# Linear attention: 64-row products side by side, and other PSUM banks for the output gate's second layer

## The reference, cut to what matters

```python
b = jnp.cumsum(log_a, axis=3)                       # within a chunk of 64 tokens
qd = q * jnp.exp(b) * (dk ** -0.5)
kd = k * jnp.exp(-b)
kl = k * jnp.exp(b_last - b)
kv = jnp.einsum('bhncd,bhnce->bhnde', kl, v)        # per chunk and head: 128 x 256, sum over 64 tokens
# s_prev[n+1] = decay[n] * s_prev[n] + kv[n]
o_inter = jnp.einsum('bhncd,bhnde->bhnce', qd, s_prev)
a = jnp.where(causal, jnp.einsum('bhncd,bhnsd->bhncs', qd, kd), 0.0)
o = o_inter + jnp.einsum('bhncs,bhnse->bhnce', a, v)
...
o_a = rms_norm(o_a, gla_out_norm) * jax.nn.silu(g_r)   # g_r: the output gate, two layers of 512 columns here
```

## Time and profile before

| what | value |
|---|---|
| median of 3 runs | 1502.66 us (1494.79, 1502.66, 1503.58) |
| the profiled execution's own time | 1496.99 us |
| its span in the trace | 1495.2 us |
| mean granted TensorE clock | 0.966 |
| PE busy | 1289.9 us (86%) |
| DVE busy | 946.0 us (63%) |
| ACT busy | 592.1 us (40%) |
| chain that ended last, by engine | PE 54%, DMA 22%, DVE 12%, ACT 8% |

### The profile page before, as it was taken

One profiled execution on the slowest core, in us unless ns is written; L12 is line 12 of the kernel. 1 busy time (PEld: TensorE's weight loads), 2 busy tenths in 40 slices (PEclk: granted clock), 3 DMA queues, 4 the chain that ended last, 5 costly groups with the idle time before them and its releaser, 6 DMA issues.

```text
span 1495.2 us, 16428 instructions
## 1 busy us (share of the span) xinstructions
PE 1289.9 (86%) x6072; PEld 909.0 (61%) x6072; DVE 946.0 (63%) x1961; ACT 592.1 (40%) x1013; POOL 279.8 (19%) x281
## 2 busy tenths in 40 slices
PE   7998999287878888787878777699899999999998
PEld 7987797243424343342424223397488899999887
DVE  5656455687776868777677765564555456766445
ACT  4455453232322223132322221463445754545334
POOL 1000000244343535443434333000000000000000
PEclk9998899699999999999999999899899999999999
DMA  7442342499999999999999999355234445555551
GB/s 268 136 149 96 113 169 89 175 423 421 421 422 421 415 422 400 421 405 422 403 422 421 421 421 422 151 209 170 85 120 162 142 144 194 167 180 185 202 190 71
DMA packets 56982, 398.78 MB, mean 267 GB/s; under 512 B 7096, under 2 KB 7352, under 8 KB 9032
## 3 DMA queue, kind: packets, MB, share of 16 engines
q0 software_dynamic: 36864, 268.45, 43.5%
q1 hardware_dynamic: 17856, 125.84, 24.2%
q10 hardware_dynamic: 2184, 3.45, 0.7%
HBM read 396.67 MB, written 1.05 MB: 266 GB/s over the span
## 4 chain that ended last, share of the span: by engine, by line
PE 54%; DMA 22%; DVE 12%; ACT 8%; issue 4%; POOL 1%; ACTq 0%; SPq 0%; DVEq 0%; POOLq 0%
PE ps L727 41%; DMA B<-in_ex,eidx 21%; PE ps L970 9%; DVE B L2001 4%; ACT hl L1195 2%; DVE hl L1675 2%; ACT diags L1435 1%; ACT av_ L1430 1%; DVE XT L1684 1%; ACT L1576 1%; ACT L1430 1%; ACT L1417 1%; POOL B L691 1%; DVE av_ L2005 1%; PE ps L930 0%
## 5 line engine op out<-in xcount | busy, mean ns | idle before, releaser
L970 PE MATMUL ps<-B,diags 128*128 128x512 f32 x1024 | 480.4, 615 | 150.0 <-ACT diags L1435 150.0
L970 PEld LDWEIGHTS ps<-B,diags 128*128 128x128 f32 x1024 | 188.9, 193 | 431.3 <-ACT diags L1435 238.5
L1675 DVE TENSOR_TENSOR hl<-ring,hl 128x2048 fp32r<-128x2048 f32 x118 | 270.1, 2291 | 262.4 <-ACT hl L1195 262.2
L691 POOL DMA_INDIRECT B<-in_ex,eidx x256 | 273.7, 1069 | 648.6 <-PE ps L970 358.1
L2001 DVE CUSTOM_DVE_ANT_0 B<-B 128x1024 f32<-128x1024 f32 x256 | 309.8, 1220 | 111.3 <-DMA B<-in_ex,eidx 111.1
L1195 ACT ACTIVATE hl<-ring 128x2048 fp32r<-128x2048 f32 x118 | 224.8, 1908 | 136.4 <-PE ps L727 135.6
L727 PE MATMUL ps<-XT,hl 128*128 128x256 f32 x2136 | 268.4, 287 | 4.2 <-DVE XT L1684 4.2
L727 PEld LDWEIGHTS ps<-XT,hl 128*128 128x128 f32 x2136 | 262.1, 194 | 9.4 <-issue 5.1
L1430 ACT ACTIVATE av_<-av_ 128x2 f32<-128x2 f32 x128 | 26.0, 203 | 430.3 <-DVE av_ L2001 430.3
L727 PE MATMUL ps<-hl,R 128*128 128x512 f32 x792 | 182.7, 391 | 0.0
L727 PE MATMUL ps<-hl,XT 128*128 128x512 f32 (+1 forms) x720 | 164.3, 389 | 7.0 <-DVE B L2086 7.0
(11 more groups left out here) (312 smaller groups left out, 875.6 us busy)
## 6 DMA issues: line engine op xcount, KB each, us to landing
ring<-in_wt SPq DMA_DIRECT2D x117, 1024.0 KB, 4.9
B<-in_ex,eidx POOLq DMA_INDIRECT x256, 13.0
X<-in_x SPq DMA_DIRECT2D x2, 512.0 KB, 4.4
B<-in_mem ACTq DMA_DIRECT2D x1, 1024.0 KB, 10.3
ring<-in_wple SPq DMA_DIRECT2D x1, 1024.0 KB, 5.0
out<-B SPq DMA_DIRECT2D x4, 256.0 KB, 2.0
GB<-in_gffn ACTq DMA_DIRECT2D x1, 512.0 KB, 3.5
GB<-in_gfin ACTq DMA_DIRECT2D x1, 512.0 KB, 4.3
```

The costliest lines, as they stand in the source:

```text
L691: e.indirect_dma_start(out=rows[i % NG][:, :], out_offset=None, in_=A["ex"], in_offset=bass.IndirectOffsetOnAxis(ap=eidx[:, tb, s:s + 1], ...
L970: m = e.matmul(acc[tb][hf][:, :], diags[:, i % 4, :], rows[i % NG][:, 1024 + 512 * hf:1536 + 512 * hf], start=(s == 0), stop=(s == 127))
L1675: e.tensor_tensor(w[1][:, :], ring[:, i % RING, :], w[0][:, :].bitcast(F32), ALU.subtract).then_inc(lo.sem)
```

## The change

Three edits in the linear attention, all on PE and in the planner; no engine other than PE gets another order, and no instruction is added or removed.

- The state products of chunks 0 and 1 are issued together, before the second half of `bq` layer 0: for each pair of heads, both banks are taken, and for each head the product of chunk 0 stands directly before that of chunk 1. `SA(2)` stays between the halves of `gr` layer 1.
- In the outputs the two intra-chunk products of a head stand directly behind each other, and then its inter-chunk products.
- In the deal of banks, two are passed over ahead of `gr` layer 1.

```diff
@@ planner, GROUPS
-        for n in range(3):
-            GROUPS += [(("SA", n, hp), sas[n, hp]) for hp in range(2)]
-            if n == 1:
-                layer_groups("gr", 1, lambda tb: grs[1, tb])
+        GROUPS += [(("SA", n, hp), sas[n, hp]) for hp in range(2) for n in range(2)]
+        layer_groups("gr", 1, lambda tb: grs[1, tb])
+        GROUPS += [(("SA", 2, hp), sas[2, hp]) for hp in range(2)]
@@ planner, the deal
+                if key == ("gr", 1, 0):
+                    turn += 2
                 while turn % 8 in held:
                     turn += 1
@@ PE
-            for n in range(3):
-                o = 64 * (n % 2)
-                for hp in range(2):
-                    ps = bank(("SA", n, hp))
-                    if n == 0 and hp == 0:
-                        e.wait_ge(*klts[1])
-                        e.wait_ge(*gvs[1, 1])
-                    for c in range(2):
-                        h = 2 * hp + c
-                        m = e.matmul(ps[:, c * 256:c * 256 + 256],
-                                     klt[o:o + 64, (n // 2) * 512 + h * 128:(n // 2) * 512 + h * 128 + 128],
-                                     gv[o:o + 64, n // 2, h * 256:h * 256 + 256], start=True, stop=True)
-                    mark(m, ("SA", n, hp))
-                if n == 0:
-                    t_half("bq", 0, 1, XT)
-                else:
-                    t_half("gr", 1, n - 1, XT)
+            def state(n, hp, c):
+                o, h = 64 * (n % 2), 2 * hp + c
+                return e.matmul(ps_of(("SA", n, hp))[:, c * 256:c * 256 + 256],
+                                klt[o:o + 64, (n // 2) * 512 + h * 128:(n // 2) * 512 + h * 128 + 128],
+                                gv[o:o + 64, n // 2, h * 256:h * 256 + 256], start=True, stop=True)
+            e.wait_ge(*klts[1])
+            e.wait_ge(*gvs[1, 1])
+            for hp in range(2):
+                for n in range(2):
+                    bank(("SA", n, hp))
+                for c in range(2):
+                    m = [state(n, hp, c) for n in range(2)]
+                for n in range(2):
+                    mark(m[n], ("SA", n, hp))
+            t_half("bq", 0, 1, XT)
+            t_half("gr", 1, 0, XT)
+            for hp in range(2):
+                bank(("SA", 2, hp))
+                for c in range(2):
+                    m = state(2, hp, c)
+                mark(m, ("SA", 2, hp))
+            t_half("gr", 1, 1, XT)
@@ PE, outputs oN(tb, hp), for each head
                         for q in range(2):
                             n, o = 2 * tb + q, 64 * q
                             m = e.matmul(ps[o:o + 64, c * 256:c * 256 + 256],
                                          AT[o:o + 64, (h * 2 + tb) * 64:(h * 2 + tb) * 64 + 64],
                                          gv[o:o + 64, tb, h * 256:h * 256 + 256], start=True, stop=(n == 0))
+                        for q in range(2):
+                            n, o = 2 * tb + q, 64 * q
                             if n:
                                 e.wait_ge(*sas[n - 1, hp])
                                 m = e.matmul(ps[o:o + 64, c * 256:c * 256 + 256],
```

More of the change, by code:

```diff
@@ L568, in program @@
         MARKS += [("klT", 0), ("klT", 1)]
-        for n in range(3):
-            MARKS += [("SA", n, hp) for hp in range(2)]
-            if n == 0:
-                t_marks("bq", 0, 1)
-            else:
-                t_marks("gr", 1, n - 1)
+        MARKS += [("SA", n, hp) for hp in range(2) for n in range(2)]
+        t_marks("bq", 0, 1)
+        t_marks("gr", 1, 0)
+        MARKS += [("SA", 2, 0), ("SA", 2, 1)]
+        t_marks("gr", 1, 1)
         MARKS += [("bT", 0, 0), ("bT", 0, 1)]
```

## The result

| | before | after |
|---|---|---|
| median of nine runs each | 1502.88 us | 1488.45 us |
| ratio after to before, 95% interval | | 0.991 [0.9891, 0.993] |
| a second timing (e0 below) | 1501.68 us | 1490.71 us, 0.9934 [0.9911, 0.9957] |
| span of the profiled execution | 1495.2 us | 1487.3 us |
| first state product to end of outputs (the stage) | 48.3 us | 36.85 us |

One of the nine runs after took 1540.20 us at a granted clock of 0.831; it counts as a slow one, and the ratio rests on the other eight.

What follows compares the result with a forecast made beforehand. PE was taken to bound the kernel; 6.4 us up to the end of `bT(0)` plus 4.6 us in the outputs gave 11.0 us, placing the time at 1490 us, own range 1484 to 1497, overall 1481 to 1500.

Steps and rivals of the forecast that it cites:

- What bounds the kernel: Whole kernel: PE's time bounds it, so PE time taken out of this stretch moves the end.
- (a) states: State products of chunks 0 and 1: row halves overlap fully, 16 instructions in 1.96 us.
- The charge for a change of tile shape at each alternation: State products: a possible penalty of about 0.09 us for each of 8 alternations, +0.7 us; full overlap was taken instead.
- `bq` behind them: Second half of `bq` layer 0 behind the states: starts at 1039.81 as before and ends at 1047.1.
- (c) the new wait: Inside `SA(2)`: 2.8 us waiting for DVE's L2111 to free `SA(1,0)`'s bank, then 1.6 us of low clock in `gr`'s half.
- (d) outputs: Token block 1 of the outputs: paired products overlap, 1.16 us a head for 2.30, 4.6 us gained over four heads.
- no overlap of states: Rival, chance 0.12: state products do not overlap, all behind comes 1.9 us later (2.6 with penalty), time 1492 to 1493.
- no overlap of output pairs: Rival, chance 0.07: output pairs of 128 rows do not overlap, 2.3 us less gain, time 1492.
- The wait that is not got rid of: Rival, chance 0.08: waiting for `SA(1,0)` behind `head_norm(0)` costs as much as the old bank wait; time 1497.
- the slower case: Rival, chance 0.05: the clock stays low behind the new hole; through the following 60 us it would end at 1520.

Runs made afterwards that it cites:

- e0: The changed kernel timed again with no edit; median 1490.71 us, ratio 0.9934 to the kernel before, stage 36.9 us.
- e4: The kernel before with two banks passed over ahead of `gr` layer 1 and nothing else; median 1490.80 us, ratio 0.9926, stage 40.8 us.
- e8: e6 with all state products reading the lower 64 partitions, results not those of the reference; block of 16 took 5.00 us.
- e3: The changed kernel with the outputs in the old order (intra, inter, intra, inter for each head); single timing 1496.19 us, stage 43.2 us.
- e5: The kernel before with two banks passed over and output products in pairs, states as before; ratio 0.9902, stage 36.2 us.
- e6: The changed kernel with the four banks of the paired states dealt by chunk; median 1482.78 us, ratio 0.9875, stage 32.5 us.
- e7: The kernel before with the output products in pairs and nothing else; single timing 1498.51 us, stage 43.8 us.
- e10: e6 with the four state products of chunk 0 issued first, then the four of chunk 1; block of 16 took 4.75 us.
- e1: The changed kernel without passing over two banks; single timing 1499.28 us, stage 41.5 us.
- e2: The changed kernel with, for each pair of heads, two state products of chunk 0, then two of chunk 1; block 2.10 us, stage 36.8 us.
- e11: e6 with the block of paired states moved behind the second half of `bq` layer 0; median 1477.28 us, ratio 0.9858.

## Why the prediction was right, point by point

The time of 1488.45 us lies 1.5 under the 1490 forecast and inside the forecast's own range. The stage was to be 37.3 us and is 36.85; its gain 11.0, and it is 11.4. The mechanism came as forecast, step by step; that the sum is so close is partly luck, as the terms show.

- **What bounds the kernel**: shown. Every edit's effect on the stage came out at the end, with tails equal to 0.2 us in all kernels. Of the five kernels timed more than once in the experiments, four have the stage's gain inside the interval of their ratio; e4's 7.5 lies 0.5 us under its own.
- **(a) states**: full overlap, 2.00 us against 1.96 taken; e8 shows that it is the row halves. The charge for a change of tile shape at each alternation did not come. The Trainium skill (TensorEngine Tiling (Array Packing), Gotcha 1) lets row tiles run together if they write different banks; with these four banks the trace agrees, and nothing was tried within one bank.
- **`bq` behind them**: predicted to end as before, after 7.28 us. It took 5.72, since the clock did not fall there. This term was mis-sized by 1.6 us, and it could have gone either way: behind the same wait of 2.2 us the clock fell in before, e3, e4, e5, e6, e7, e8 and e10, and not in after, e0, e1 and e2.
- **(c) the new wait**: its place, releaser and size were right, 3.1 us for 2.8, and so was the clock behind it for the half layer (7.33 for 7.3). The low clock already covered the four instructions ahead of that: 2.07 for 1.1. This and `bq` nearly cancel, which is luck: had the clock fallen in `bq` as before, the stage would be about 38.4 us and its gain 9.9.
- **(d) outputs**: 0.58 us for L1078 x4, as L1009 had promised; e3 and e7 give 4.5 and 4.5 for 4.6. By the rule of the Trainium skill that the prediction names (TensorE: Matmul & The Clock Gate, Part 3, The mechanism), weight loads overlap products only across row groups, and 2.3 us would have been left. The trace does not agree with it here either: L1078 x4 shares all rows, and its four took 0.58 us.
- **The rivals**: no overlap of states (e8: 5.00 us as run, an estimated 3.7 at the full clock) and no overlap of output pairs did not come. The wait that is not got rid of is e1, not the change; the 1497 named for it is 1496.4 by its own terms. The clock came back at about 1064.3 (0.50 up to 1064, 0.96 over 1064 to 1068), so the slower case did not come.
- **What the prediction did not see**: it worked out the change as a whole and never set its parts against each other. The banks alone take 7.5 us off the stage as run (e4), 9.1 with the clock of before; with the outputs it is 12.1 as run, more than the 11.4 of the whole change (e5). The states' 1.9 us are less than the 3.1 us wait that their order of banks brings.

Open stays whether the limit of three that PE goes past is one of products, of loads and products, or of something else, and what decides whether the clock falls behind the 2.2 us wait.

## What to carry to other kernels

When an engine waits for a buffer that a round-robin deal has given it, look at who holds each of the buffers at that moment, and deal the one that was read first. After an edit to the order, do the same again: here the new order put a late holder under an urgent result, and its wait of 3.1 us is more than the 1.9 us that the pairing saved. Put the products that need a copy behind a block that needs nothing, so that the copy is covered; in the one profile of it, this also kept the clock up.

## What the runs showed of the hardware that was not expected

PE took up state products of the upper 64 rows while three instructions ahead of them in the program had not begun on the lower rows (e2: 16 in 2.10 us), but not while four had not (e10). The Trainium skill (TensorE: Matmul & The Clock Gate, Part 3, The mechanism) says that products start in program order. The 2.10 us don't agree: with starts in order, e2's four, four, four and four would need about 12 x 0.216 + 0.3 = 2.9 us, by the same estimate.

Behind one and the same wait of 2.2 us the clock fell in eight profiles and stayed at 1.00 in four; where it fell, it did so in some among the state products (2.97 us for eight in e4, 1.96 in before) and in others only in the layer behind them. That makes single profiles differ by 1.6 us where the program up to there is the same: states and `bq` took 9.24 us before and 10.85 in e4. In e11, where the wait is gone, the clock stayed at 1.00 through the stage.
